# Second block's attention on one core: values of one query tile at a time, and scores issued two passes ahead of the last turns

## The reference, cut to what matters

```python
# 8 heads of 64, 2 key/value heads, queries in tiles of 128, 512 keys
# N_SELECT 16 blocks of 64 keys are chosen of only 8, and WINDOW is 512,
# so that both branches see all keys up to the query
s = jnp.einsum('bqkgd,bqknrd->bqkgnr', qc, kg)      # selected branch, keys ks
p = masked_softmax(s, mask)
o_slc = jnp.einsum('bqkgm,bqkmd->bqkgd', p, vg)
s_win = jnp.einsum('bcqkgd,bcmkd->bckgqm', qw, kw)  # window branch, keys kw
p_win = masked_softmax(s_win, win_mask)
o_win = jnp.einsum('bckgqm,bcmkd->bcqkgd', p_win, vw)
g = jax.nn.sigmoid(g_raw + gate_b)
o = g[:, :, 0] * o_cmp + g[:, :, 1] * o_slc + g[:, :, 2] * o_win
```

## Time and profile before

| what | value |
|---|---|
| median of 3 runs | 1986.96 us (1983.17 to 1992.41) |
| span of the profiled execution | 1982.0 us |
| PE busy | 1873.8 us, 95% of the span |
| DVE, ACT, POOL busy | 959.8, 523.0, 332.9 us |
| the stretch of the change | 1448.6 to 1532.4 us |
| in it: PE, DVE, ACT, POOL busy | 72.69, 58.89, 53.51, 29.11 us |

### The profile page before, as it was taken

The page is one execution under the profiler, slowest core; times in us unless marked ns, Lnnn a source line. Parts: engine busy times, 40 slices in busy tenths (PEclk is TensorE's granted clock), DMA queues, the critical chain, the costliest instruction groups (busy, mean ns, idle before and its releaser), DMA issues. The chain is left out here.

```text
span 1982.0 us, 27981 instructions
## 1 busy us (share of the span) xinstructions
PE 1873.8 (95%) x10606; PEld 1040.9 (53%) x10606; DVE 959.8 (48%) x2029; ACT 523.0 (26%) x1154; POOL 332.9 (17%) x297
## 2 busy tenths in 40 slices
PE   8999999999998999999999998999988999999997
PEld 3434448845443344444444443457745588888443
DVE  4987748732375232332332335623375554444643
ACT  2448831101311233333333332220255100000000
POOL 0655530000027110010010014300023000000000
PEclk9999999999999999999999999999999999999999
DMA  6129972204355999999999999613310122222311
GB/s 249 64 80 231 230 217 99 81 5 152 145 195 170 359 406 405 403 402 404 407 407 405 400 402 372 239 68 118 128 43 1 43 105 87 85 85 85 129 62 43
DMA packets 85535, 396.88 MB, mean 200 GB/s; under 512 B 13394, under 2 KB 13650, under 8 KB 60240
## 3 DMA queue, kind: packets, MB, share of 16 engines
q1 hardware_dynamic: 55728, 303.59, 40.1%
q10 hardware_dynamic: 16880, 58.52, 10.2%
q0 software_dynamic: 12848, 33.74, 4.7%
HBM read 374.66 MB, written 55.09 MB: 217 GB/s over the span
## 5 line engine op out<-in xcount | busy, mean ns | idle before, releaser
L2823 DVE COPY slab<-bank 32x512 f32<-32x512 f32 x124 | 80.8, 688 | 400.2 <-PE bank L1476 400.2
L1089 PE MATMUL bank<-ring,slab 128*128 128x512 f32 (+1 forms) x608 | 254.6, 578 | 6.5 <-DVE slab L2291 3.8
L1468 PE MATMUL bank<-slab 128*32 128x512 f32 x1536 | 228.9, 599 | 17.1 <-DMA ring<-w_exp_down 6.6
L1468 PE MATMUL bank<-ring,slab 128*32 128x512 f32 x1536 | 228.5, 598 | 14.6 <-DVE slab L2779 5.1
L1476 PE MATMUL bank<-ring,slab 128*32 128x512 f32 x512 | 228.5, 599 | 0.0
L1476 PE MATMUL bank<-slab 128*32 128x512 f32 x480 | 214.0, 599 | 0.0
L1089 PEld LDWEIGHTS bank<-ring,slab 128*128 128x128 f32 x608 | 115.7, 192 | 139.1 <-issue 130.4
L3225 POOL TENSOR_TENSOR small<-small 128x1 f32<-128x1 f32 (+2 forms) x30 | 27.5, 920 | 817.1 <-DVE small L2288 817.1
L1468 PEld LDWEIGHTS bank<-slab 128*32 128x32 f32 x1536 | 73.5, 110 | 145.7 <-issue 139.8
L1089 PE MATMUL bank<-slab,ring 128*128 128x512 f32 (+1 forms) x368 | 148.2, 559 | 1.7 <-ACT slab L1831 0.9
L1468 PEld LDWEIGHTS bank<-ring,slab 128*32 128x32 f32 x1536 | 72.3, 110 | 144.9 <-issue 142.2
(11 more groups left out here) (363 smaller groups left out, 3053.7 us busy)
## 6 DMA issues: line engine op xcount, KB each, us to landing
ring<-stream SPq DMA_DIRECT2D x173, 512.0 KB, 4.4
slab<-w_exp_gu SPq DMA_DIRECT2D x64, 1024.0 KB, 13.8
ring<-w_exp_gu SPq DMA_DIRECT2D x64, 1024.0 KB, 13.6
ring<-w_exp_down SPq DMA_DIRECT2D x32, 1024.0 KB, 22.3
slab<-w_exp_down SPq DMA_DIRECT2D x32, 1024.0 KB, 23.0
y_rows<-zeros ACTq DMA_DIRECT2D x1, 24960.0 KB, 132.0
y_rows<-slab ACTq DMA_DIRECT2D x64, 384.0 KB, 8.2
gb<-rows ACTq DMA_DIRECT2D x5, 512.0 KB, 4.4
```

What stands on the lines that cost most here:

```text
L1089: mm = nc.tensor.matmul(dst, lhs[k], rhs[k], start=(k == 0), stop=(k == len(lhs) - 1))
L1468: mm = nc.tensor.matmul(g_bank[32 * g:32 * g + 32, :], x[:, k, 32 * g:32 * g + 32], w[:, 512 * k:512 * k + 512], start=(k == 0), stop=(k = ...
L2823: i = nc.vector.tensor_copy(ye[b % 2][32:64, 512 * half:512 * half + 512], bank[5 + half][96:128, :])
```

## The change

PE's loop has one more iteration. The values are split by query tile: `nsa_values(w, q)` takes the 2 (q + 1) matmuls of tile q and waits only for the copies of the turns that hold them; the compressed part becomes a function of its own. A turn waits for exactly the scalings that it reads. In iteration w PE issues scores 0 and 1 of w, the values of tile 3 of w - 3, scores 2 and 3, turns 2 and 3 of w - 2, scores 4 to 7, the compressed part, the values of tiles 0 and 1 of w - 2, turn 4, the values of tile 2, and turns 0 and 1 of w - 1. DVE's scalings of w - 1 are spread between the masks of w: scaling 3 now comes after `fac_ready` is raised, and scaling 5 after masks 6 and 7. ACT's order follows. POOL is unchanged.

```diff
@@ psum_order @@
-    for m in range(4):
-        add("s2", m, "dve")
-    for w in range(NW + 2):
...
+    for w in range(NW + 3):
+        if w < NW:
+            for m in range(2):
+                add("s2", 8 * w + m, "dve")
+        if w >= 4 and w % 2 == 0:
+            add("o2", (w - 4) // 2, "act")
...
@@ -1127,33 +1121,35 @@
                         tile("s2", 8 * w + m)[:, 0:(q + 1) * P])
 
             def nsa_turn(w, m):
-                q = NEED_Q[m] - 1
-                pe.wait_ge(scaled_dve, 6 * w + 2 * min(q, 2) + 2)
-                if q == 3:
-                    pe.wait_ge(scaled_pool, 2 * w + m - 2 if m >= 3 else 2 * w)
+                if m < 3:
+                    pe.wait_ge(scaled_dve, 6 * w + (3, 5, 6)[m])
+                else:
+                    pe.wait_ge(scaled_pool, 2 * w + m - 2)
                 turn("pt2", 5 * w + m, [nsa_p(w, j, q, k, k + 1) for j, q, k in nsa_blocks[4 * m:4 * m + 4]])
 
-            def nsa_values(w):
+            def nsa_compressed(i):
+                dst = tile("o2", i)
+                free("o2", i)
+                for j in range(2):
+                    nc.tensor.matmul(dst[64 * j:64 * j + 64, :], vcR[32 * i:32 * i + 32, j, :],
+                                     pcT[32 * i:32 * i + 32, j, :], start=True, stop=False)
+
+            def nsa_values(w, q):
                 i, br = w // 2, w % 2
-                evac("pt2", 5 * w + 2)
-                evac("pt2", 5 * w + 4)
+                for m in ((0,), (0, 1), (1, 2), (3, 4))[q]:
+                    evac("pt2", 5 * w + m)
                 dst = tile("o2", i)
-                if br == 0:
-                    free("o2", i)
+                for k in range(q + 1):
                     for j in range(2):
-                        nc.tensor.matmul(dst[64 * j:64 * j + 64, :], vcR[32 * i:32 * i + 32, j, :],
-                                         pcT[32 * i:32 * i + 32, j, :], start=True, stop=False)
-                for q in range(NT):
-                    for k in range(q + 1):
-                        for j in range(2):
-                            at = 128 * br + 64 * j
-                            b = tri_at(j, q, k)
-                            mm = nc.tensor.matmul(dst[64 * j:64 * j + 64, q * P:(q + 1) * P], vsw[:, k, at:at + 64],
-                                                  nsa_pT(w, b, b + P), start=False, stop=(br == 1 and q == NT - 1 and k == q))
-                if br == 0:
-                    mm.then_inc(values_done, 1)
-                else:
-                    close(mm, "o2", i)
+                        at = 128 * br + 64 * j
+                        b = tri_at(j, q, k)
+                        mm = nc.tensor.matmul(dst[64 * j:64 * j + 64, q * P:(q + 1) * P], vsw[:, k, at:at + 64],
+                                              nsa_pT(w, b, b + P), start=False, stop=(br == 1 and q == NT - 1 and k == q))
+                if q == NT - 1:
+                    if br == 0:
+                        mm.then_inc(values_done, 1)
+                    else:
+                        close(mm, "o2", i)
 
             for i in range(4):
                 need("u", i)
@@ -1647,32 +1643,31 @@
             pe.wait_ge(gate_ready, SIGS + KD + 2)
             evac("vcc", 0)
             evac("pct", 3)
-            for m in range(4):
-                nsa_scores(0, m)
-            for w in range(NW + 2):
+            for w in range(NW + 3):
+                if w < NW:
+                    for m in range(2):
+                        nsa_scores(w, m)
+                if w >= 3:
+                    nsa_values(w - 3, 3)
+                if w < NW:
+                    for m in range(2, 4):
+                        nsa_scores(w, m)
+                if 2 <= w < NW + 2:
+                    for m in range(2, 4):
+                        nsa_turn(w - 2, m)
+                if w < NW:
+                    for m in range(4, 8):
+                        nsa_scores(w, m)
+                if 2 <= w < NW + 2:
+                    if w % 2 == 0:
+                        nsa_compressed((w - 2) // 2)
+                    for q in range(2):
+                        nsa_values(w - 2, q)
+                    nsa_turn(w - 2, 4)
+                    nsa_values(w - 2, 2)
                 if 1 <= w <= NW:
-                    nsa_turn(w - 1, 0)
-                if w < NW:
-                    for m in range(4, 6):
-                        nsa_scores(w, m)
-                if 1 <= w <= NW:
-                    for m in range(1, 3):
+                    for m in range(2):
                         nsa_turn(w - 1, m)
-                if w < NW:
-                    for m in range(6, 8):
-                        nsa_scores(w, m)
-                if 1 <= w <= NW:
-                    nsa_turn(w - 1, 3)
-                if w + 1 < NW:
-                    for m in range(2):
-                        nsa_scores(w + 1, m)
-                if w >= 2:
-                    nsa_values(w - 2)
-                if 1 <= w <= NW:
-                    nsa_turn(w - 1, 4)
-                if w + 1 < NW:
-                    for m in range(2, 4):
-                        nsa_scores(w + 1, m)
             evac("o2", 3)
             pe.wait_ge(squares_ready, 2)
             free("sb", 0)
@@ -2216,27 +2211,27 @@
                         full("o2", (w - 2) // 2)
                 nc.scalar.activation(nsa_pT(w, 512 * m, 512 * m + 512), tile("pt2", 5 * w + m)[:, :], ACT.Copy).then_inc(act_evac, 1)
 
-            for w in range(NW + 2):
+            for w in range(NW + 3):
                 if w < NW:
-                    for m in range(4):
+                    nsa_exp(w, 0)
+                if w >= 4 and w % 2 == 0:
+                    i = (w - 4) // 2
+                    full("o2", i)
+                    nc.scalar.activation(fm(bsq, i), tile("o2", i)[:, :], ACT.Square).then_inc(bsq_ready, 1)
+                    nc.scalar.activation(fm(bT, i), tile("o2", i)[:, :], ACT.Copy, scale=col("out_b", i)).then_inc(act_evac, 1)
+                if w < NW:
+                    for m in range(1, 5):
+                        nsa_exp(w, m)
+                if 2 <= w < NW + 2:
+                    nsa_turned(w - 2, 3)
+                    nsa_turned(w - 2, 4)
+                if w < NW:
+                    for m in range(5, 7):
                         nsa_exp(w, m)
                 if 1 <= w <= NW:
                     nsa_turned(w - 1, 1)
                 if w < NW:
-                    for m in range(4, 6):
-                        nsa_exp(w, m)
-                if 1 <= w <= NW:
-                    nsa_turned(w - 1, 3)
-                if w < NW:
-                    for m in range(6, 8):
-                        nsa_exp(w, m)
-                if w >= 2 and w % 2 == 1:
-                    i = (w - 3) // 2
-                    full("o2", i)
-                    nc.scalar.activation(fm(bsq, i), tile("o2", i)[:, :], ACT.Square).then_inc(bsq_ready, 1)
-                    nc.scalar.activation(fm(bT, i), tile("o2", i)[:, :], ACT.Copy, scale=col("out_b", i)).then_inc(act_evac, 1)
-                if 1 <= w <= NW:
-                    nsa_turned(w - 1, 4)
+                    nsa_exp(w, 7)
 
             def half_turned(i):
                 full("h4T", i)
@@ -3017,27 +3012,37 @@
                 nc.vector.tensor_copy(nsa_pT(w, 512 * m, 512 * m + 512), tile("pt2", 5 * w + m)[:, :]).then_inc(dve_evac, 1)
 
             dve.wait_ge(mask_ready, 1)
-            for w in range(NW + 1):
+            for w in range(NW + 2):
+                scaling = 1 <= w <= NW
                 if w < NW:
-                    for m in range(4):
+                    for m in range(3):
                         nsa_mask(w, m)
-                if w >= 1:
+                if scaling:
+                    link(nsa_factor(w - 1, 0))
+                if w < NW:
+                    nsa_mask(w, 3)
+                if scaling:
+                    for m in range(2):
+                        nsa_scale(w - 1, m)
+                if w >= 2:
+                    nsa_turned(w - 2, 2)
+                if w < NW:
+                    nsa_mask(w, 4)
+                if scaling:
+                    nsa_scale(w - 1, 2)
+                if w < NW:
+                    nsa_mask(w, 5)
+                if scaling:
                     nsa_factor(w - 1, 1).then_inc(fac_ready, 1)
+                    nsa_scale(w - 1, 3)
                     dve.wait_ge(fac_ready, w)
-                    for m in range(4, 6):
-                        nsa_scale(w - 1, m)
-                    nsa_turned(w - 1, 0)
-                if w < NW:
-                    for m in range(4, 6):
-                        nsa_mask(w, m)
-                if w >= 1:
-                    nsa_turned(w - 1, 2)
+                    nsa_scale(w - 1, 4)
                 if w < NW:
                     for m in range(6, 8):
                         nsa_mask(w, m)
-                    link(nsa_factor(w, 0))
-                    for m in range(4):
```

(43 more changed lines are left out.)

14 lines of the change are left out of this document (6 added, 8 removed).

## The result

The changed kernel takes 1977.5 us (median of 10 runs, 1973.3 to 1980.4) against 1988.1 (10 runs), a ratio of 0.9949, 95% interval 0.9935 to 0.9964. A second set of runs gave 0.9950 (0.9931 to 0.9969); one more run of that set took 6902 us with the clock at 1.0, for a reason that stays unknown, and is counted nowhere. So it is about 10 us faster, where 6.4 were forecast: the direction and the range were right, the gain was a good third too small.

The account below looks back on a forecast made before the run. TensorE's chain bounds the kernel, standing about 13.3 us in the stretch for DVE, fill and drain. Stands 6.7 + 3.4 + 3.2 become 0 + 3.9 + 2.0, plus 0.8 for group ends: 6.4 us less, 1980.6 us, range 1974 to 1988.

Parts of the forecast that it names:

- the mechanism of the old stand: In each full pass TensorE stands 1.12 us ahead of turn 1, waiting for DVE, which had waited for TensorE.
- nothing is late in full passes: Longest new loop, turn 4 through DVE's masks, scale 5 and copy 0 to turn 2: 7.5 us against 8.4, 0.9 spare.
- DVE, ACT and POOL hide: Per pass, DVE about 8.0 us, ACT 6.1 to 7.2 and POOL 3.33 stay under TensorE's 8.4 or 9.4.
- the stretch: From the first score to the product of the sums: 83.72 us before, 77.5 us expected after.
- The clock's rival: More, smaller groups make the clock fall in the passes: 4.8 us slower, 1992 us; chance 0.05.
- Full passes: Iterations 3 to 7 on TensorE without stand: three of 8.4 and two of 9.4 us, 44.0 in all.
- the upper bound of what I allowed: Splitting the values into three groups on TensorE costs 0 to 0.3 us a pass.
- Fill: First passes: turn 2 of pass 0 goes at 1460.7 us, with 3.9 us of TensorE stand, then work to 1468.1.
- DVE's load: DVE's work in a full pass: 7.34 + 0.43 = 7.8 us, about 8.0 with handovers.
- Drain: Last passes without scores: 11.5 us of work, stands of 0.57, 0.14 and 1.33, 13.6 us with group ends.
- Rival 2: All stand goes, in the fill too: best case 10 us less, 1977 us; chance 0.11.
- a sign of being wrong: More than one fall in the clock row after the change would show the forecast wrong.

Follow-up runs that it names:

- number 2: Kernel before, with the values of a pass moved whole between scores 4, 5 and turn 1, old waits: ratio 0.9998, stretch 84.61 and 81.40 us.
- number 7: Changed kernel with four more 384-column DVE instructions a pass ahead of scaling 5: ratio to before 1.0012, stretch 85.73 us.
- number 1: Kernel before, its order kept, with turns waiting only for the scalings they read: ratio 1.0001, stretch 83.87 us.
- the repeat: The changed kernel profiled once more with no edit: stretch 72.51 us, 451.3 us from there to the end.
- number 3: Changed kernel with each pass's values whole again, early, between scores 0, 1 and 2, 3: ratio to before 0.9971, stretch 78.86 us.
- number 4: Changed kernel with each pass's values whole again, late, between scores 4 to 7 and turn 4: ratio to before 0.9972, stretch 76.70 us.
- number 9: As number 2, with matmuls adding nothing put into TensorE's four largest stands outside full passes: ratio to before 0.9988, stretch 79.86 us.

## Why the prediction came out a third too small

What held: the mechanism of the old stand and that it goes; that nothing is late in full passes; that DVE, ACT and POOL hide; that a microsecond before 1534 us arrives at the end (449.6 us behind the stretch in the profiles with no fall of the clock there). The clock's rival did not come in: the changed kernel loses 28.4 us to it, before 28.5. What the Trainium skill, "TensorE: Matmul & The Clock Gate", section "A second HAM failure mode: psum-queue depth-cycling", tells of, a clock that swings with small idles between groups, is not seen here: with three groups of values for one the clock stayed at 1.00 in the stretch, and the falls in numbers 2 and 7 came outside the full passes, behind stands of 0.6 to 2.6 us.

The stretch was forecast at 77.3 us and is 72.5. The 4.8 are three mis-sized terms:

- *Full passes*, 44.0 forecast, 1511.39 - 1469.23 = 42.2 measured, 1.8 of the 4.8. I took each pair of turns at 1.25 us from the earlier trace rows as work. But 0.23 of it was turn 2's wait for the copy of turn 0 (number 1); a pair takes 1.02 when the bank is free. The stand ahead of it is not what makes it dear: right behind a stand of 0.83 the row of a pair is 1.06 us long, that of the earlier trace rows 1.32. Two pairs a pass make 0.45. Scores 4 to 7 in one group take 1.70 and not 1.89. Against that the three groups of values cost 2.65 and not 2.33: the price of splitting, 0.3 us a pass, is at the upper bound of what I allowed.
- *Fill*, 19.5 against 17.4: 2.0. From DVE's first mask of pass 1 (1455.90) to the end of its copy of turn 0 (1462.16) it is 6.3 us, where I gave a full iteration, 7.8. There is no copy of turn 2 yet (0.6), and DVE's load was too high: 7.2 in a full pass, where I had 7.8. Those two make 1.2 of the 1.5, and the other 0.3 I can't place; what is left of the 2.0 is the same turns and scores as above.
- *Drain*, 13.8 against 12.9: 0.9. The stand of 0.57 ahead of turn 2 of pass 6 hung on scaling 5 at 0.85 us, which takes 0.42 there, and the 0.14 for ACT's copy did not come.

So what the prediction had wrong in size is the price of work: a wait of 0.23 us was read as part of each pair of turns, and DVE's queue was taken 0.6 us a pass too dear. The account of the kernel before was off by the same wait: a pass stood 1.12 and 0.23 us, not 1.12 alone.

Rival 2 named 1977 us, and 1977.5 came. That is luck for it: it let all stand go with the work unchanged, but by the prices above some 2.8 us of stand is left in the fill (an estimate: 10.5 us to turn 2 of pass 0, with 7.7 of work in them), and what makes up for it is cheaper work. Of what I said would be seen, three things did not come so: the stands ahead of turns 1 and 2 of pass 0 are 0.70 and 0.34 us and not 1 to 1.5, there is none in the drain, and the clock falls twice, which I had named as a sign of being wrong; both falls are behind the stretch, and the repeat has one. I gave 0.17 to a gain of over 0.5%; the two ratios lie on that line.

In the profiles 1.7 of the 11.2 us is the clock's fall inside the old stretch. Over all runs the changed kernel loses as much to the clock as before, so at an equal clock the profiles show 9.5 us; the ratios give 10, and the medians 10.6 and 11.3, within the intervals.

What I weighed wrongly besides is the split: I gave it no gain at all. Numbers 3 and 4 show that without it about half of the gain is lost, most of that (in number 4) at the two ends.

## What to carry to other kernels

When an engine waits for a queue that waits for that engine, put other work between the question and the answer; loosening the wait alone shows the next one behind it, here a PSUM bank. A row of a timeline can hold a wait that no bracket shows, when two waits end close together: before a duration goes into a sum as work, compare it with the same instructions at another place of the trace. Small pieces paid less in the full loop here (1.5 of 4.2 us) than in its first and last turns, where whole blocks leave nothing to slip in.

## What the runs showed of the hardware

- The granted clock can take back what a better order gives: 3.4 us in number 2, after stands of 0.6 to 1.8 us, while passes with a stand of 1.04 in every 9.4 kept 1.00. When the stands inside were filled (number 9), the fall came behind the stretch. Not every such stand is followed by a fall: the changed kernel has 1.50 and 0.70 at its beginning and kept 1.00 there in both profiles. What decides where it comes was not settled.
- A 384-wide scaling on DVE takes 0.85 or 0.42 us while POOL works, and POOL's own instruction differs with it. In the changed kernel scaling 4 starts 0.08 or 0.09 us behind POOL's first scaling in all eight passes. In three it takes 0.84 or 0.85 us and POOL's 1.60; in five it takes 0.41 and POOL's 1.84 or 1.85, and the repeat has the same in the same passes:

```profile
1475.30 1.60 POOL L3385 TENSOR_SCALAR work<-work,s5x 128x512 f32<-128x512 f32 x1 [5.68 <-DVE s5x L2286]
```

```profile
1500.39 1.85 POOL L3385 TENSOR_SCALAR work<-work,s5x 128x512 f32<-128x512 f32 x1 [4.55 <-DVE s5x L2286]
1500.48 0.41 DVE L2283 TENSOR_SCALAR work<-work,s5x 128x384 f32<-128x384 f32 x1
```

So one of the two takes 0.25 to 0.44 us more, and the distance of the starts does not tell which; the rule was not found. (POOL's spans are rough in these profiles.)
